# Four steps of a gated linear attention head stand elsewhere in the engines' orders

## What is computed

```python
def decay(f_pre):
    f = lb + (1.0 - lb) * jax.nn.sigmoid(f_pre.astype(F32))
    return _bht(_heads(1.0 - f, HG_HEADS)), _bht(_heads(jnp.log(f), HG_HEADS))
...
b = jnp.cumsum(lfc, axis=2)
o = jnp.einsum('bhtk,bhkv->bhtv', qc * jnp.exp(b), S)
pair = jnp.exp(jnp.where(tri, b[:, :, :, None, :] - b[:, :, None, :, :], -jnp.inf))
a = jnp.einsum('bhtk,bhtsk->bhts', qc, pair * kc[:, :, None, :, :])
o = o + jnp.einsum('bhts,bhsv->bhtv', a, vc)
...
o = _rms(jnp.swapaxes(o, 1, 2).astype(z.dtype), h_norm.reshape(HG_HEADS, HG_VDIM))
return (o.reshape(o.shape[:2] + (HG_VW,)) * jax.nn.silu(z)) @ w_out
```

## Time and profile before

| | |
|---|---|
| median of 3 runs | 3653.43 us (3652.62 to 3655.23) |
| profiled execution, its own time | 3655.55 us |
| its span in the trace | 3653.7 us |
| PE (TensorE matmul) busy | 3503.1 us, 96% |
| DVE (VectorE) | 1924.9 us, 53% |
| ACT (ScalarE) | 1136.2 us, 31% |
| POOL (GpSimd) | 859.8 us, 24% |
| mean share of the 16 DMA engines | q1: 16.7% |

### The profile page before, as it was taken

One profiled execution on the slowest core, in us unless ns is written; L12 is line 12 of the kernel. 1 busy time (PEld: TensorE's weight loads), 2 busy tenths in 40 slices (PEclk: granted clock), 3 DMA queues, 4 the chain that ended last, 5 costly groups with the idle time before them and its releaser, 6 DMA issues.

```text
span 3653.7 us, 53450 instructions
## 1 busy us (share of the span) xinstructions
PE 3503.1 (96%) x22170; PEld 2308.8 (63%) x22170; DVE 1924.9 (53%) x3502; ACT 1136.2 (31%) x2145; POOL 859.8 (24%) x704
## 2 busy tenths in 40 slices
PE   7999999999999999999999999999999999999998
PEld 4555555665668776666666657444455544878887
DVE  3555553345545344666666654354777743454543
ACT  3443442222231213332233320775445421010000
POOL 2212121222210003444434420232444430000000
PEclk9999999999999999999999999999999999999999
DMA  5121111101111121111111021222010011312221
GB/s 224 64 81 67 68 51 46 46 35 35 35 71 71 67 75 47 48 47 37 46 47 47 30 84 53 82 76 74 31 48 30 34 59 61 115 70 92 85 80 55
DMA packets 29551, 229.73 MB, mean 63 GB/s; under 512 B 3072, under 2 KB 6784, under 8 KB 9728
## 3 DMA queue, kind: packets, MB, share of 16 engines
q1 hardware_dynamic: 29312, 226.33, 16.7%
HBM read 224.22 MB, written 2.10 MB: 62 GB/s over the span
## 4 chain that ended last, share of the span: by engine, by line
PE 82%; DVE 8%; ACT 4%; issue 3%; POOL 2%; DMA 1%; SPq 0%; DVEq 0%; ACTq 0%; POOLq 0%
PE bank L1284 12%; PE bank L1503 7%; PE bank L1951 7%; PE bank L1610 5%; PE bank L1978 4%; PE bank L1606 3%; PE bank L1730 3%; PE bank L1569 3%; PE bank L1689 2%; PE bank L1869 2%; PE bank L1409 2%; PE bank L1696 2%; PE bank L1442 2%; PE bank L1231 2%; PE bank L1915 2%
## 5 line engine op out<-in xcount | busy, mean ns | idle before, releaser
L1284 PE MATMUL bank<-xT,ring 128*128 128x384 f32 x896 | 323.5, 494 | 2.6 <-ACT Y L2093 2.4
L3603 POOL TENSOR_TENSOR ring<-ring 128x512 f32<-128x512 f32 x112 | 146.8, 1328 | 413.0 <-DMA ring<-in_w 411.3
L1284 PE MATMUL bank<-hT,ring 128*128 128x384 f32 x672 | 242.8, 493 | 0.0
L1284 PEld LDWEIGHTS bank<-xT,ring 128*128 128x128 f32 x896 | 161.3, 190 | 108.3 <-issue 15.3
L3641 POOL TENSOR_TENSOR ring<-ring 128x512 f32<-128x512 f32 x96 | 134.5, 1407 | 319.0 <-DMA ring<-in_w 318.9
L3667 POOL TENSOR_TENSOR arena<-arena 128x512 f32<-128x512 f32 x112 | 159.9, 1428 | 208.0 <-PE bank L1659 207.9
L1730 PE MATMUL bank<-hT,ring 128*128 128x512 f32 x384 | 178.9, 599 | 4.7 <-ACT Y L2068 4.7
L1610 PE MATMUL bank<-Y,ring 128*128 128x384 f32 x512 | 183.2, 497 | 0.0
L1284 PEld LDWEIGHTS bank<-hT,ring 128*128 128x128 f32 x672 | 121.4, 190 | 80.8 <-issue 16.0
L1610 PE MATMUL bank<-hT,ring 128*128 128x384 f32 x384 | 138.1, 496 | 10.1 <-DVE arena L3042 9.3
L3093 DVE TENSOR_TENSOR arena<-arena 128x512 f32<-128x512 f32 x112 | 129.0, 1152 | 30.8 <-PE bank L1659 30.8
(11 more groups left out here) (590 smaller groups left out, 7579.3 us busy)
## 6 DMA issues: line engine op xcount, KB each, us to landing
ring<-in_w SPq DMA_DIRECT2D x77, 1024.0 KB, 4.8
ring<-in_w SPq DMA_DIRECT2D x35, 2048.0 KB, 8.0
ring<-in_w SPq DMA_DIRECT2D x20, 1280.0 KB, 5.7
ring<-in_w SPq DMA_DIRECT2D x10, 1536.0 KB, 6.6
ring<-in_w SPq DMA_DIRECT2D x8, 1408.0 KB, 5.9
ring<-in_w SPq DMA_DIRECT2D x6, 512.0 KB, 3.4
xT<-in_xT SPq DMA_DIRECT2D x1, 3072.0 KB, 14.8
xT<-in_xT SPq DMA_DIRECT2D x4, 512.0 KB, 6.8
```

The costliest lines, as they stand in the source:

```text
L1284: ins = e.matmul(bank[spot["st", kind, n, at]][:, 0:384], left[:, k], right[:, k], start=first and k == 0, stop=k == 3, skip_group_check=True)
L3603: e.tensor_tensor(s[:, i], l, r, op).then_inc(up("st_s", (kind, n, i)), 1)
```

## The change

No instruction is added or taken away, and none changes its shape. Four kinds of steps stand elsewhere in the list:

1. The block totals of a level are a step of their own, `gl_w(j, li)`. It stands ahead of `gl_m(j, li)`, one tick behind `gl_x(j, li)`: behind the masked copy a(li - 1) and the `gs_r` adds of the filler in between.
2. The weight sums stand three chunks later (`n + 5 + 3 * i` for `n + 2 + 3 * i`), which is one sum's distance; the fourth now falls into chunk 0 of what follows.
3. The queries' products: the first head's one chunk later, the second head's from the last query chunk to chunk 1 of the f unit behind it. The decays `gl_g` go from chunks 0 and 1 behind their f unit to chunks 1 and 3 (1 and 2 where queries follow).
4. `gl_y(j - 1)` goes from ahead of m(1) of head j to behind a(1), with level 2's step.

```diff
 def gl_queries(n):
     made = [[("gl_q", j, c)] for j in (2 * n, 2 * n + 1) for c in range(4)]
-    made[5].append(("gl_qd", 2 * n))
-    made[7].append(("gl_qd", 2 * n + 1))
+    made[6].append(("gl_qd", 2 * n))
     return made
...
         for li in range(1, 7):
-            yield [[("gl_x", j, li)] + [("gl_p", j, li)] * (li < 5) + [("gl_a", j, li - 1)], [("gl_m", j, li)]]
-        yield [[("gl_x", j, 7), ("gl_a", j, 6)]]
+            first = [("gl_x", j, li)] + [("gl_p", j, li)] * (li < 5) + [("gl_a", j, li - 1)] + [("gl_y", j - 1)] * (li == 2 and j > 0)
+            yield [first, [("gl_w", j, li), ("gl_m", j, li)]]
+        yield [[("gl_x", j, 7), ("gl_a", j, 6)], [("gl_w", j, 7)]]
         yield [[("gl_t", j, 0)], [("gl_u", j, 0)]]
-        yield [[("gl_t", j, 1)], [("gl_u", j, 1)], [("gl_o", j)], [("gl_n", j)], [("gl_y", j)]]
+        yield [[("gl_t", j, 1)], [("gl_u", j, 1)], [("gl_o", j)], [("gl_n", j)], [("gl_y", j)] * (j == 15)]
...
-            for at_, step in enumerate(late):
-                chunks[at_].append(step)
-            late = [("gl_g", n, 1), ("gl_g", n, 0)] if kind == "f" else []
+            for chunk, step in late:
+                chunks[chunk - (kind == "q" and chunk == 3)].append(step)
+            late = {"f": [(1, ("gl_g", n, 1)), (3, ("gl_g", n, 0))], "q": [(1, ("gl_qd", 2 * n + 1))], "v": []}[kind]
...
         for i, step in enumerate(gs_sums(*kind)):
-            filler[n + 2 + 3 * i][1].append(step)
+            filler[n + 5 + 3 * i][1].append(step)
...
                 e.tensor_tensor(o, o, gl_total(m, 0, m), ALU.mult).then_inc(up("gl_high", (j, li)), 1)
+
+            def gl_w(j, li):
+                m = 1 << (li - 1)
                 q.wait_ge(*on("gl_high", (j, li)))
                 q.wait_ge(*on("gl_low", (j, li)))
```

More of the change, by code:

```diff
@@ L390, in gl_steps @@
         t, group = next(filler, (0.0, None))
-    made += late
+    made += [step for _, step in late]
     side = iter(gl_last())
@@ L3568, in vector @@
                   "na_r": na_r, "na_y": na_y, "ml_gate": ml_gate, "ml_r1": ml_r1, "ml_r2": ml_r2, "ml_e": ml_e, "ml_x": ml_x,
-                  "ml_a": ml_a, "ml_hb": ml_hb, "ml_hd": ml_hd, "ml_og": ml_og, "ml_yd": ml_yd, "oab": oab, "oab_t": oab_t, "oab_u": oab_u, "oc": oc, "oc7": oc7, "sv_begin": sv_begin, "gl_bound": gl_bound, "gs_t": gs_t, "gs_r": gs_r, "gl_t": gl_t, "gl_qd": gl_qd, "gl_g": gl_g,
+                  "ml_a": ml_a, "ml_hb": ml_hb, "ml_hd": ml_hd, "ml_og": ml_og, "ml_yd": ml_yd, "oab": oab, "oab_t": oab_t, "oab_u": oab_u, "oc": oc, "oc7": oc7, "sv_begin": sv_begin, "gl_bound": gl_bound, "gs_t": gs_t, "gs_r": gs_r, "gl_t": gl_t, "gl_w": gl_w, "gl_qd": gl_qd, "gl_g": gl_g,
                   "gl_i": gl_i, "gl_c": gl_c, "gl_u": gl_u, "gl_d2": gl_d2, "gl_x": gl_x, "gl_a": gl_a,
```

## The result

The median fell from 3653.43 us (3652.62 to 3655.23, 3 runs) to 3612.29 us (3611.45 to 3612.86, 3 runs). The ratio is 0.9886 with a 95% interval of [0.9864, 0.9909], so the changed kernel is 41.1 us faster. The forecast was 3621.4 us, 32 us faster, and its range ended at 3615 us: the time lies 2.7 us outside of it. The direction was right, and the size was too small by 9.1 us.

A forecast was written before the change was run, and what follows sets the result against it. PE bounds the GLA part, with 45.1 us of gaps as the most to win. Closing four waits gives 7.4 + 9.3 + 5.2 + 11.3 = 33.2 us, less 1.2 for rests: 32 us faster, 3621.4 us, range 3615 to 3635 us.

The forecast's parts named there:

- the deduction: 1.2 us taken off for rests, since three level products of each period have two chunks of filler against 2.76 us.
- C: Wait of 0.39 us at m(1) of the odd head, its pack behind the reciprocal root; forecast to stay, 2.7 us.
- E: Wait of 1.61 us at direction 1's update of the odd head; the decays' move closes it, 11.3 us.
- B: Wait of 1.31 us at block product 6 of the even head's f unit; the totals' move closes it, 9.3 us.
- A: Wait of 0.96 us at m(4) of the even head; the later weight sums close it, 7.4 us.
- D: Wait of 0.75 us at m(2) of the odd head; moving queries' product and output closes it, 5.2 us.
- Rival 1: DVE starts first at more levels, low ends 0.63 us later, new pack waits: 3627 to 3634 us; chance 0.22.
- the rule that the prediction weighed: DVE with two SBUF inputs and POOL exclude each other; low takes 1.78 us with DVE first, 1.15 otherwise.
- 2 (the gaps move): Closed waits reappear where slack was little: 3642 us, or 3649 us with A not closed; chance 0.10.
- 3 (slower): Totals held by POOL's sums make the next low late at 64 places: 3665 to 3701 us; chance 0.05.
- rival 4: C closes too, or unlisted short waits go: 3618 us, or 3608 us with all 45.1 us gone; chance 0.05.

The follow-up runs named there:

- decays alone: The kernel before with only the decays moved, behind chunks 1 and 3: 3639.40 us, ratio 0.9959.
- sums alone: The kernel before with only the weight sums moved three chunks later: 3643.33 us, ratio 0.9970.
- the root's kernel: The changed kernel with ACT's reciprocal root of the output put behind pack(1) of the next head: 3609.30 us, ratio 0.9877 to the kernel before.
- output alone: The kernel before with only the output's scaling and gate moved behind a(1) of the next head: 3653.32 us, ratio 0.9994.
- totals alone: The kernel before with only the block totals made a step of their own, behind the masked copy and the adds: 3651.46 us, ratio 0.9992.
- without the sums: The changed kernel with the weight sums back two chunks behind their unit's start: 3625.91 us, ratio 0.9919 to the kernel before.
- the second comparison: The changed kernel itself, unedited, measured again beside the kernel before: 3612.30 us against 3654.54 us, ratio 0.9882.

## Why the size was wrong

**Where the 41.1 us are.** The forecast summed the idle time: 7.4 + 9.3 + 5.2 + 11.3 = 33.2 us, less 1.2. Measured in the part:

| | us |
|---|---|
| idle time of PE that is gone, 45.1 - 11.6 | 33.5 |
| what closed waits gave beside their idle time (the remainder) | 4.8 |
| the stretch at half clock | 1.7 |
| the part, 743.9 - 703.9 | 40.0 |
| rest of the program, 41.1 - 40.0 (medians less traces) | 1.1 |

The forecast was 9.1 us short: 4.8 for what closed waits gave beside their idle time, 1.7 for the half clock, 1.2 for the deduction, 1.1 outside the part and 0.3 of idle time. With the first added and the deduction left out it would have been 3615.4 us, just inside its range; the 1.7 and 1.1 us made the rest, and no run here shows their cause.

**The sum of the gaps** was right: 33.5 us for 33.2. All four closed, C stayed, and no new wait of 0.3 us opened.

**The step that failed** is the first sentence on the change, that each part "is worth what its chain gives back, up to its gap", with the gaps' idle time as the bound. "45.1 us of it are gaps, and no edit of this kind can win more" has the same error. A gap's idle time is not its price. Where PE doesn't wait, the next product starts before the row of the last one ends, and behind a wait it can't. At E the overlap is 1670.91 - 1670.75 = 0.16 us, and the update itself takes 0.83 us where it took 0.94 us behind its wait, together 0.27 us. (The profile models the ends of PE's rows. The starts alone say the same: from the filler's start to the update's it is 4.45 us before and 2.68 us after, 1.77 us less for an idle time of 1.61.) At B it is 1616.89 - 1616.73 = 0.16 us, and the product takes 1.45 us for 1.56, again 0.27 us. At A it is 1605.88 - 1605.81 and at D 1645.94 - 1645.87, 0.07 us each, with the same 0.46 us for the level product. For 15 waits of the B and E kind and 14 of A and D that makes 15 x 0.27 + 14 x 0.07 = 5.0 us. One level product of the changed kernel starts 0.13 us behind the row ahead of it (at 2021.53 us), where others start 0.07 us before its end; less these 0.20 us it is the 4.8 us measured. The single moves bear the two sizes out: 0.28 us for each closed E (decays alone), 0.05 us for each closed A (sums alone), 0.07 us for each closed C. The 0.17 us that I expected for every kind, for the single moves and for the root's kernel, were wrong; the overlap depends on the products on both sides. The rows for it stood in the trace of before, at every place where PE didn't wait.

**The half clock** was not in the sum at all; the prediction read "full granted clock" from the 1.00 of the earlier trace rows, which is 1 - 1.7/830 = 0.998, rounded. That it was in 4 of 4 traces of before and 0 of 3 of the changed kernel speaks against chance alone, though seven traces are few. A long wait of PE stands ahead of every stretch, but most long waits have none behind them, so what sets it off is not settled. In two of the four traces of before the wait is the last head's, which the changed kernel has as well, so that this stretch can't be put down to a closed wait. Of the other kernels it is once in the part with the decays alone and with the output alone, three times with the totals alone, twice without the sums, and not at all with the sums alone, although that kernel keeps all eight waits of the keys. The 1.7 us are counted as measured, their cause is open.

**The 1.2 us for rests** were a deduction without an event. The level products that I feared for ran without a wait, but for the one at 2021.53 us. At A the chain was shorter than the 2.76 us of the sum: low(4) ended 1604.87 - 1603.10 = 1.77 us behind m(3), the pack at 1605.60, and with the 0.14 us behind it the chain takes 2.64 us, while m(4) started at 2.71 us, by the filler. The 1.90 us were read at low(3), and at m(3) of the odd head they came out: low(3) ends 1.90 us and m(3) starts 2.77 us behind m(2) (1646.33 to 1649.10 us), with no wait. Rival 1 is answered with it. DVE does win the start now: high takes 848 ns on average for 1152 before, low 1647 ns, the totals 717 ns.

```profile
L3670 POOL TENSOR_TENSOR arena<-arena 128x512 f32<-128x512 f32 x112 | 184.4, 1647 | 212.7 <-PE bank L1659 195.6 <-DVE arena L3100 17.1
L3093 DVE TENSOR_TENSOR arena<-arena 128x512 f32<-128x512 f32 x112 | 95.0, 848 | 100.8 <-PE bank L1659 99.3
```

POOL's low took 1428 ns on average before. It is slower by 0.22 us for each, and no wait of PE opened by it. The rows agree with the rule that the prediction weighed (the Trainium skill, SBUF — State Buffer, SBUF: two separate sides), that the first to start keeps the lock for a whole instruction: DVE, 0.05 us earlier at 1603.17, runs at its usual 0.69 us, and low is held. The size in the prediction was off, because it set 1.78 us at low(3) against 1.15 us at low(4). Level by level low(3) takes 1.78 us behind DVE and 1.27 us ahead of it, low(4) 1.65 and 1.15 us: 0.50 us, not 0.63. A low held from its own start to high's end would lose 0.64 us, so the trace agrees with the rule to 0.14 us.

**Attribution** was wrong in two places while the sum came out.

- E was given to the decays. The totals alone close it as well: without total(7) ahead of it, the add that ACT's sigmoid waits for ends earlier, and the second decay, which still waits 1.58 us for ACT, is 2.2 us earlier against the filler. The decays' move gives 13.0 us of the part where it is alone and 0.2 us in company.
- D was given to the queries and the output together. The output's move adds 0.1 us to the others. The queries' move is a condition for the totals': without it total(1) is stuck behind the queries' product, a wait that the prediction looked for at low(3), behind total(2), and not at low(2). The totals alone, with 9.3 us in my sum, have an interval that contains no change; their part is 6.5 us shorter, with 5.1 us of half clock in it for 1.7.

**Outside the part** 1.1 us remain, and 2 us if the second comparison is taken (42.2 us by the medians, 40.0 to 40.6 us in the part). Ahead of the part the stretches at half clock cost 8.5 to 12.0 us in the seven traces of the two kernels and differ from one execution to the next. Behind it before took 1502.8 to 1503.9 us in four traces and the changed kernel 1502.6 us in three. What makes these 0.2 to 1.3 us stays open.

**The rivals.** 2 (the gaps move) and 3 (slower) did not occur in the full change. 2 did occur in "totals alone", where D took back much of what B and E had given, and in "output alone", where 0.57 us at m(3) took the place of 0.75 us at m(2). The number of rival 4 came nearest (3618 us with C closed, 3608 us with all gaps gone), but by luck: C was not closed, and the idle time that went was that of the forecast.

## What to carry on

Price a closed wait as its idle time plus what the same pair of instructions shows where nothing waits: how far the next row starts ahead of the end of the last, and how much shorter it is. Deduct nothing for "rests" without a named place. And when several moves act on one queue, cost them as sets as well as alone: here one move closed what another was credited with, and opened a wait that only a third one's move closed.

## What the runs showed of the hardware

- A product behind a wait costs PE more than its idle time: 0.27 us at products of 128x384 and 128x128 in float32, 0.07 us at level products of 128x32. It is the same to 0.01 us at all places of a kind, but for the one with a stretch at half clock behind it.
- When DVE and POOL wait for the same product, DVE starts 0.04 to 0.05 us earlier (1614.16 and 1614.20, 1641.94 and 1641.99) and POOL's low beside it then takes 0.50 us longer than where POOL was first: 1.78 for 1.27 us at level 3, 1.65 for 1.15 us at level 4.
- DVE's masked copy of a PSUM bank and its add of a bank take 0.73 and 0.53 us beside a running low on POOL (1614.20 to 1615.76): they were not held. Over the GLA part the masked copy takes 724 ns on average for 721 ns before, and the add 552 ns for 545.
- Each of the 11 stretches at half clock in the part, over 18 traces, begins 0.1 to 1.4 us behind the start of a product that had waited 1.79 to 2.75 us; 22 waits of that length have none behind them.
